# A column step of 144 instead of 128 in the gathered rows' two parts

## The chip, the cores and the metric

The kernel runs on one core of a Trainium2 chip. The metric is device time in microseconds (us), the median of several runs; lower is better. TensorE (PE) multiplies, and its weight loads are a row of their own in the profile (PEld). VectorE (DVE), ScalarE (ACT) and GpSimd (POOL) work on vectors, SyncE (SP) issues most transfers.

## The reference

One inference step of a decoder with two layers, for a prompt of 256 tokens and eight sample tokens (264 token columns), 1024 channels, float32. Layer 0 is a pooling mixer and a dense SwiGLU; a shared key and value projection follows; layer 1 is dilated attention and a mixture of eight SwiGLU experts, of which each token uses two. The change lies in the last part:

```python
def moe_swiglu(h, w_router, b_router, w1, w3, w2):
    ...
    for e in range(N_EXPERTS):
        y = swiglu(h, w1[e], w3[e], w2[e]).astype(jnp.float32)
        out = out + dense_gate[..., e:e + 1] * y
```

`swiglu` is `(silu(h @ w1) * (h @ w3)) @ w2`. An expert has two matrices of 1024 x 3584 and one of 3584 x 1024.

## The kernel before, in words

**Buffers.** Each buffer is placed by `sb`, one behind the other along the partition, its length rounded up to 64 bytes. A ring of seven slabs of 2048 columns takes the weights from memory (1 MB each). `w_hi` and `w_lo` have three slabs each of the same size. `tT` and its like hold 8 x 264 columns. `phase` has 12840 columns and is used by one stage after the other: `at` and `over` give names to parts of it.

**Split products.** Every float32 product is made of two parts of each operand. ACT rounds a weight slab from the ring into `w_hi` (L1266 for the experts), DVE writes the remainder into `w_lo` (L1734), and the helper `three` (L476 to L478) multiplies high by high, high by low and low by high into one sum: three matmuls, each with its own weight load. "Triple" is used below for these three.

**The expert stage.** For each expert a transfer on POOL's queue brings its 128 gathered rows (`xg`), PE transposes them in eight chunks of 128 columns (`turn_rows`, L907), ACT writes the high part `xe_hi` out of PSUM in two instructions of four chunks each (`gathered_high`, L1291), and DVE the remainder `xe_lo` (`gathered_low`, L1823). For the next expert this is done before the last products of the present one. Then, for each of seven column blocks j, `product` is called twice, for w1 and w3: eight chunks k, for each one triple with `xe_hi[:, k, :]` or `xe_lo[:, k, :]` as stationary operand and 512 columns of a weight slab as moving operand, all into one PSUM bank. `down` makes the product with w2 for the block before, with `upT_hi` and `upT_lo` (in `tT`) stationary, and alternates between two PSUM banks triple by triple. `turn` (L933) transposes the block `up` for it.

```python
                        for i in range(4):
                            k = 4 * half + i
                            mm = three(bank[bk][0:SLOTS, :], (xe_hi[:, k, :], xe_lo[:, k, :]), (hi[:, i, :], lo[:, i, :]), k == 0, k == KC - 1)
```

**Order and waits.** PE waits for `lo_done` of a slab; ACT waits for PE to be done with the slab whose place in `w_hi` it takes (`pair_used`); DVE waits for ACT; SP's transfer into a ring slot waits for DVE. At the start of an expert PE waits for `xe_ready`, which DVE gives after `xe_lo`.

**Earlier stages** use the same helper with the weights stationary and 264 token columns moving: `tHi` and `mLo` (8 chunks that stand 264 columns, 1056 bytes, apart), while the stationary slices `hi[:, k, ...]` stand 256 columns apart.

Of the kernel before, what the change touches and what calls it, by code (L numbers as in the profile page):

```python
# [6 lines left out]
F32R = mybir.dt.float32r  # L7
I32 = mybir.dt.int32
# [4 lines left out]
P = 128  # L13
D = 1024
KC = D // P
T = 256
NB = 8
# [10 lines left out]
NE = 8  # L28
# [7 lines left out]
SLOTS = 128  # L36
# [61 lines left out]
def yoco_step(nc, w, o):  # L98
# [25 lines left out]
    with ExitStack() as ctx:  # L124
# [3 lines left out]
        def sb(name, shape, dt=F32):  # L128

            n = 4  # L130
            for x in shape[1:]:
                n *= x
            placed[name] = free[0]
            free[0] += -(-n // 64) * 64
            return nc.alloc_sbuf_tensor_at(name, shape, dt, offset=placed[name])

        def over(name, other, skip, shape, dt):

            return nc.alloc_sbuf_tensor_at(name, shape, dt, offset=placed[other] + 4 * skip)
# [50 lines left out]
        phase = sb("phase", [P, PHASE])  # L190

        def at(offset, *shape):
            n = 1
            for s in shape:
                n *= s
            assert offset + n <= PHASE, (offset, shape)
            v = phase[:, offset:offset + n]
            if len(shape) == 2:
                v = v.rearrange("p (a b) -> p a b", a=shape[0])
            if len(shape) == 3:  # L200
                v = v.rearrange("p (a b c) -> p a b c", a=shape[0], b=shape[1])
            if len(shape) == 4:
                v = v.rearrange("p (a b c d) -> p a b c d", a=shape[0], b=shape[1], c=shape[2])
            return v
# [58 lines left out]
        htok = at(0, 3, D)  # L263
        x2tok = at(3072, 3, D)
        gtok = at(6144, 2, D)
        xe_hi = over("xe_hi", "phase", 8192, [P, KC, SLOTS], F32R)
        xe_lo = over("xe_lo", "phase", 9216, [P, KC, SLOTS], F32R)
        xg = hflat[:, 0:D]
        ye = mflat[:, 0:D]
        gsel = mflat[0:1 + NB, D:D + P]  # L270
        grow = at(10240, D)[0:1 + NB, :]

        upT_hi = [over(f"upT_hi{i}", "tT", 1024 * i, [P, 4, P], F32R) for i in range(2)]
        upT_lo = [over(f"upT_lo{i}", "tT", 1024 * i + 512, [P, 4, P], F32R) for i in range(2)]
        up_s = at(10240, 512)
        up = at(10752, 512)
        lg = at(11264, 3, NE)
        sel = at(11288, 3, NE)
        rank = at(11312, 3, NE)
        r_c = at(11336, 3, NE)  # L280
        gate = at(11360, 3, NE)
        picks = at(11384, 2, 3, NE)
        rowbase = at(11432, NE)
        rowsum = at(11440, 2, 3)
        r_s = at(11448, 3, 4)
        gpair = at(11464, 2, 3)
        r_a = at(11472, 3, NE, NE)
        r_b = at(11664, 3, NE, NE)
        row = over("row", "phase", 11864, [P, 2, 2, 3], I32)
        tail_s = at(11880, 3, 4)  # L290
        r_d = at(11896, 2, 3)
        rb_strip = at(11904, 1)

        pickT = over("pickT", "ada", 0, [P, NT], F32)[:, :]
        pick = at(11906, 3, P)
        xflat = xT[:, :, :].rearrange("p a b -> p (a b)")
        part = [xflat[:, 0:D], xflat[:, D:2 * D], over("part_s", "const", 0, [P, D], F32)[:, :]]
        early = [hflat[:, 0:D], hflat[:, D:2 * D]]
# [1792 lines left out]
```

## Time and profile before

| | us |
|---|---|
| median of 3 runs | 1690.21 (1689.18 to 1691.46) |
| the profiled execution | 1692.17 |
| its span, first to last instruction | 1689.9 |
| PE busy in the span | 1586.1 (94%) |
| DVE busy | 1256.4 (74%) |
| ACT busy | 982.8 (58%) |

A matmul's row has its start and a modelled end; neighbouring matmuls overlap in the rows, so the pace of PE is read from start to start, not from durations. The expert stage begins at about 705 us of the span and ends at about 1669.

### The profile page before, as it was taken

The numbers are of one execution on the slowest core, as the hardware profiler recorded it, in microseconds if no ns is written. First come the engines' busy times: TensorE is split into PE (matmuls) and PEld (weight loads), VectorE is DVE, ScalarE is ACT, GpSimd is POOL, SyncE is SP. The second block draws the span as 40 slices with busy tenths as digits, with TensorE's granted clock in tenths as the row PEclk, the third lists the DMA queues.
The fourth block names the chain that finished last, engine by engine and source line by source line (L and its number), as shares of the span: only waits on it lengthen the run. The fifth ranks groups of instructions, "written<-read, shape, count | busy, mean of one in ns | idle before, by whom it ended". The sixth has DMA issues, their size and how long they took to land.

```text
span 1689.9 us, 22932 instructions
## 1 busy us (share of the span) xinstructions
PE 1586.1 (94%) x8697; PEld 1296.3 (77%) x8697; DVE 1256.4 (74%) x1097; ACT 982.8 (58%) x885; POOL 152.2 (9%) x135
## 2 busy tenths in 40 slices
PE   6889999799899887799999999999999999999996
PEld 3579999498786674488888888888888888888874
DVE  4355543578784734488898888888888888889996
ACT  2244432433323524377877877877877877777774
POOL 0000000025542401200000000000000000000210
PEclk9789999899999888699999999999999999999998
DMA  9895545855458429599999999999999999999991
GB/s 346 296 345 178 178 158 187 295 179 187 162 206 302 151 75 350 199 333 380 358 395 385 357 395 381 365 385 374 376 389 370 377 376 374 385 375 373 394 387 48
DMA packets 248253, 512.28 MB, mean 303 GB/s; under 512 B 9045, under 2 KB 68613, under 8 KB 248175
## 3 DMA queue, kind: packets, MB, share of 16 engines
q1 hardware_dynamic: 241015, 490.27, 80.8%
q0 software_dynamic: 4768, 16.89, 2.5%
q10 hardware_dynamic: 2400, 4.17, 0.7%
q8 instruction: 45, 0.74, 0.2%
q14 instruction: 25, 0.20, 0.0%
HBM read 498.19 MB, written 13.82 MB: 303 GB/s over the span
## 4 chain that ended last, share of the span: by engine, by line
PE 77%; DVE 9%; DMA 4%; POOL 3%; ACT 3%; issue 3%; SPq 1%; DVEq 0%; ACTq 0%; POOLq 0%
PE wide L476 23%; PE wide L477 22%; PE wide L478 22%; DVE w_lo L1734 2%; POOL phase L1912 2%; DMA ring<-in_ada_mix_w 2%; DVE phase L1574 2%; DMA ring<-in_ada_ffn_w 1%; PE wide L933 1%; POOL phase L1918 1%; ACT w_hi L1266 1%; PE wide L527 1%; SPq L439 1%; PE wide L538 1%; PE wide L757 1%
## 5 line engine op out<-in xcount | busy, mean ns | idle before, releaser
L1734 DVE TENSOR_TENSOR w_lo<-ring,w_hi 128x2048 fp32r<-128x2048 f32 x336 | 767.6, 2290 | 113.9 <-ACT w_hi L1266 112.7
L1266 ACT ACTIVATE w_hi<-ring 128x2048 fp32r<-128x2048 f32 x336 | 643.5, 1919 | 216.0 <-PE wide L478 214.3
L476 PE MATMUL wide<-w_hi,xe_hi 128*128 128x512 f32 x896 | 356.0, 397 | 5.6 <-DVE w_lo L1734 2.9
L478 PE MATMUL wide<-w_hi,xe_lo 128*128 128x512 f32 x896 | 350.3, 391 | 0.0
L477 PE MATMUL wide<-w_lo,xe_hi 128*128 128x512 f32 x896 | 349.9, 391 | 0.0
L476 PE MATMUL wide<-tHi,w_hi 128*128 128x264 f32 x672 | 198.3, 295 | 20.4 <-DVE mLo L1492 20.4
L406 DVE TENSOR_TENSOR w_lo<-ring,w_hi 128x2048 fp32r<-128x2048 f32 (+1 forms) x58 | 139.6, 2410 | 100.1 <-ACT w_hi L1005 99.8
L477 PE MATMUL wide<-mLo,w_hi 128*128 128x264 f32 x736 | 212.1, 288 | 0.0
L476 PEld LDWEIGHTS wide<-w_hi,xe_hi 128*128 128x128 f32 x896 | 168.9, 189 | 44.9 <-DVE w_lo L1734 8.6
L478 PEld LDWEIGHTS wide<-w_hi,xe_lo 128*128 128x128 f32 x896 | 168.7, 188 | 36.1
L477 PEld LDWEIGHTS wide<-w_lo,xe_hi 128*128 128x128 f32 x896 | 169.0, 189 | 33.3
L478 PE MATMUL wide<-tHi,w_lo 128*128 128x264 f32 x672 | 192.8, 287 | 0.0
L476 PE MATMUL wide<-w_hi,upT_hi 128*128 128x512 f32 x448 | 177.1, 395 | 0.0
L477 PE MATMUL wide<-w_lo,upT_hi 128*128 128x512 f32 x448 | 176.0, 393 | 0.0
L478 PE MATMUL wide<-w_hi,upT_lo 128*128 128x512 f32 x448 | 174.3, 389 | 0.0
L476 PEld LDWEIGHTS wide<-tHi,w_hi 128*128 128x128 f32 x672 | 129.2, 192 | 30.2 <-issue 30.0
L1005 ACT ACTIVATE w_hi<-ring 128x2048 fp32r<-128x2048 f32 (+1 forms) x58 | 109.2, 1885 | 61.2 <-PE wide L478 61.1
L477 PEld LDWEIGHTS wide<-mLo,w_hi 128*128 128x128 f32 x736 | 141.9, 193 | 0.3
L478 PEld LDWEIGHTS wide<-tHi,w_lo 128*128 128x128 f32 x672 | 128.9, 192 | 0.0
L478 PEld LDWEIGHTS wide<-w_hi,upT_lo 128*128 128x128 f32 x448 | 84.1, 188 | 19.0
L476 PEld LDWEIGHTS wide<-w_hi,upT_hi 128*128 128x128 f32 x448 | 84.1, 188 | 18.3
L477 PEld LDWEIGHTS wide<-w_lo,upT_hi 128*128 128x128 f32 x448 | 84.3, 188 | 16.5
(313 smaller groups left out, 1711.6 us busy)
## 6 DMA issues: line engine op xcount, KB each, us to landing
ring<-in_moe_w SPq DMA_DIRECT2D x336, 1024.0 KB, 7.4
ring<-in_ffn_w SPq DMA_DIRECT2D x30, 1024.0 KB, 5.4
ring<-in_ada_mix_w SPq DMA_DIRECT2D x24, 1024.0 KB, 8.7
ring<-in_ada_ffn_w SPq DMA_DIRECT2D x24, 1024.0 KB, 11.9
ring<-in_w_q SPq DMA_DIRECT2D x12, 1024.0 KB, 9.2
ring<-in_cache_k SPq DMA_DIRECT2D x24, 512.0 KB, 5.0
ring<-in_cache_v SPq DMA_DIRECT2D x24, 512.0 KB, 6.5
ring<-in_w_kv SPq DMA_DIRECT2D x8, 1024.0 KB, 6.3
```

Source lines behind the costliest of these rows:

```text
L406: eng.tensor_tensor(w_lo[:, i % PAIRS, 0:size], ring[:, n % RING, 0:size], w_hi[:, i % PAIRS, 0:size].bitcast(F32), ALU.subtract).then_inc ...
L439: sp.dma_start(slab_view(n), slab_source(item)).then_inc(slab_in[n % RING], 16)
L476: pe.matmul(out, a[0], b[0], start=start, stop=False, skip_group_check=True)
L477: pe.matmul(out, a[0], b[1], start=False, stop=False, skip_group_check=True)
L478: return pe.matmul(out, a[1], b[0], start=False, stop=stop, skip_group_check=True)
L527: mm = pe.matmul(out[32 * k:32 * (k + 1), :], c32[:, 4 * half + k, :], slab_view(n)[:, k, :], start=(half == 0), stop=(half == 1))
L538: mm = pe.matmul(bank[7][:, 0:NT], ones, tT[:, k, :], start=(k == 0), stop=(k == KC - 1))
L1005: act.activation(w_hi[:, i % PAIRS, 0:size], ring[:, n % RING, 0:size], ACT.Copy).then_inc(hi_done, 1)
L1266: act.activation(w_hi[:, (NSPLIT + k) % PAIRS, :], ring[:, slot, :], ACT.Copy).then_inc(hi_done, 1)
L1574: ins = dve.tensor_tensor(k_prod[t % 2][:, cols], slab_view(n)[:, t % 2, cols], bank[6 + q], ALU.mult)
L1734: dve.tensor_tensor(w_lo[:, i, :], ring[:, slot, :], w_hi[:, i, :].bitcast(F32), ALU.subtract).then_inc(lo_done, 1)
L1912: pool.tensor_tensor(out, rawT[:, r % 4, :], cos, ALU.mult).then_inc(cos_done, 1)
```

## The change

`xe_hi` and `xe_lo` keep their shape, 8 chunks of 128 columns, but are cut from tiles with 144 columns to a chunk, so that chunk k begins 576 k bytes behind the first instead of 512 k. `xe_lo` and all that lies behind it in `phase` is moved up to make room; `xe_hi` begins where it did. `phase` keeps its size.

```diff
-        xe_hi = over("xe_hi", "phase", 8192, [P, KC, SLOTS], F32R)
-        xe_lo = over("xe_lo", "phase", 9216, [P, KC, SLOTS], F32R)
+        xe_hi = over("xe_hi", "phase", 8192, [P, KC, SLOTS + 16], F32R)[:, :, 0:SLOTS]
+        xe_lo = over("xe_lo", "phase", 9344, [P, KC, SLOTS + 16], F32R)[:, :, 0:SLOTS]
...
-        grow = at(10240, D)[0:1 + NB, :]
+        grow = at(10496, D)[0:1 + NB, :]
...
-        up_s = at(10240, 512)
-        up = at(10752, 512)
-        lg = at(11264, 3, NE)
...
+        up_s = at(10496, 512)
+        up = at(11008, 512)
+        lg = at(11520, 3, NE)
...
-        row = over("row", "phase", 11864, [P, 2, 2, 3], I32)
...
+        row = over("row", "phase", 12120, [P, 2, 2, 3], I32)
...
-        pick = at(11906, 3, P)
+        pick = at(12162, 3, P)
```

The places that are left out move by the same 256 columns.

## Rows read from the trace of the kernel before

**Rows 1.** The page, chain that ended last: by engine, by line.

```profile
PE 77%; DVE 9%; DMA 4%; POOL 3%; ACT 3%; issue 3%; SPq 1%; DVEq 0%; ACTq 0%; POOLq 0%
PE wide L476 23%; PE wide L477 22%; PE wide L478 22%; DVE w_lo L1734 2%; POOL phase L1912 2%; DMA ring<-in_ada_mix_w 2%; DVE phase L1574 2%; DMA ring<-in_ada_ffn_w 1%; PE wide L933 1%; POOL phase L1918 1%; ACT w_hi L1266 1%; PE wide L527 1%; SPq L439 1%; PE wide L538 1%; PE wide L757 1%
```

**Rows 2.** Windows, one per expert: busy time of each engine, granted clock, DMA share.

```profile
core 0: us, PE busy (x) PEld busy (x) DVE busy (x) ACT busy (x) POOL busy (x), PEclk, DMA share, GB/s
...
834.62:954.07 119.45, 119.20 (x542) 98.03 (x541) 105.64 (x60) 91.25 (x62) 1.08 (x2) 1.00 1.03 381
...
1551.30:1669.00 117.70, 115.94 (x520) 94.38 (x518) 104.62 (x62) 82.11 (x54) 19.24 (x10) 1.00 0.86 325
```

**Rows 3.** Waits in the second expert, 835 to 954 us.

```profile
engine line waited for: us in total, times, longest us
POOL y_rows L2009 <- DVE mT L1861: 129.3, 1, 129.3
ACT w_hi L1266 <- PE wide L478: 26.5, 37, 0.9
DVE w_lo L1734 <- ACT w_hi L1266: 14.1, 31, 1.2
...
PEld wide L476 <- DVE w_lo L1734: 0.9, 2, 0.7
...
PE wide L476 <- DVE w_lo L1734: 0.3, 1, 0.3
```

**Rows 4.** By tile, `xe_hi` and `xe_lo`: counts and durations.

```profile
engine op xcount: duration ns min/median/max, first and last start us, forms
L476 PE MATMUL wide<-w_hi,xe_hi x896: 389/389/791, 709.6 to 1656.1; 128*128 128x512 f32 x180
L477 PE MATMUL wide<-w_lo,xe_hi x896: 387/389/632, 710.2 to 1656.3; 128*128 128x512 f32 x180
L1291 ACT ACTIVATE xe_hi<-wide x16: 576/589/598, 707.0 to 1544.4; 128x512 fp32r<-128x512 f32 x16
L1823 DVE TENSOR_TENSOR xe_lo<-wide,xe_hi x16: 681/684/692, 708.1 to 1546.8; 128x512 fp32r<-128x512 f32 x16
...
L478 PE MATMUL wide<-w_hi,xe_lo x896: 388/389/632, 710.6 to 1656.6; 128*128 128x512 f32 x180
```

**Rows 5.** Timeline: start us, us, engine line operation; PE's transposes of gathered rows.

```profile
825.16 1.03 PE L907 MATMUL wide<-const,hT 128*128 128x128 f32 x8
```

**Rows 6.** Groups by line and form, expert stage: busy us, mean ns, idle before.

```profile
L907 PE MATMUL wide<-const,hT 128*128 128x128 f32 x56 | 7.2, 272 | 0.0
```

**Rows 7.** Groups by line and form, whole span, ACT and DVE.

```profile
L1154 ACT ACTIVATE phase<-wide 128x264 f32<-128x264 f32 x32 | 10.8, 389 | 53.4 <-PE wide L478 53.3
...
L1272 ACT ACTIVATE phase<-wide 128x256 f32<-128x256 f32 x8 | 3.1, 385 | 4.4 <-PE wide L849 4.1
...
L1273 ACT ACTIVATE phase<-wide 8x128 f32<-8x128 f32 x8 | 2.0, 250 | 0.0
...
L1377 DVE COPY phase<-wide 128x120 f32<-128x120 f32 x8 | 1.9, 283 | 1.2 <-PE wide L498 1.2
...
L1458 DVE COPY vec<-wide 128x96 f32<-128x96 f32 x1 | 0.3, 257 | 0.0
```

**Rows 8.** Timeline, boundary between the first and second expert.

```profile
827.18 1.07 ACT L1291 ACTIVATE xe_hi<-wide 128x512 fp32r<-128x512 f32 x2
...
829.52 1.28 DVE L1823 TENSOR_TENSOR xe_lo<-wide,xe_hi 128x512 fp32r<-128x512 f32 x2
...
831.30 0.19 PEld L476 LDWEIGHTS wide<-w_hi,xe_hi 128*128 128x128 f32 x1
```

**Rows 9.** Timeline of PE, settled product with `xe`: four triples apart.

```profile
835.62 0.39 PE L476 MATMUL wide<-w_hi,xe_hi 128*128 128x512 f32 x1
...
838.34 0.39 PE L476 MATMUL wide<-w_hi,xe_hi 128*128 128x512 f32 x1
```

**Rows 10.** Timeline of PE, product with `upT`: six triples apart.

```profile
826.72 0.39 PE L476 MATMUL wide<-w_hi,upT_hi 128*128 128x512 f32 x1
...
830.84 0.39 PE L476 MATMUL wide<-w_hi,upT_hi 128*128 128x512 f32 x1
```

**Rows 11.** Timeline of PE, 264 columns, layer 0: neighbouring triples.

```profile
201.41 0.28 PE L476 MATMUL wide<-tHi,w_hi 128*128 128x264 f32 x1
...
201.76 0.28 PE L476 MATMUL wide<-tHi,w_hi 128*128 128x264 f32 x1
...
202.13 0.29 PE L476 MATMUL wide<-tHi,w_hi 128*128 128x264 f32 x1
```

**Rows 12.** Timeline of PE, product with `xe` after a wait: successive triples.

```profile
840.12 0.50 PE L476 MATMUL wide<-w_hi,xe_hi 128*128 128x512 f32 x1 [0.25 <-DVE w_lo L1734]
...
840.92 0.40 PE L476 MATMUL wide<-w_hi,xe_hi 128*128 128x512 f32 x1
...
841.61 0.39 PE L476 MATMUL wide<-w_hi,xe_hi 128*128 128x512 f32 x1
...
842.30 0.39 PE L476 MATMUL wide<-w_hi,xe_hi 128*128 128x512 f32 x1
...
842.98 0.39 PE L476 MATMUL wide<-w_hi,xe_hi 128*128 128x512 f32 x1
```

**Rows 13.** Timeline of PE, 264 columns, query projection: eleven triples apart.

```profile
339.74 0.28 PE L476 MATMUL wide<-tHi,w_hi 128*128 128x264 f32 x1
...
343.73 0.28 PE L476 MATMUL wide<-tHi,w_hi 128*128 128x264 f32 x1
```

More of the change, by code:

```diff
@@ L270, in yoco_step @@
         gsel = mflat[0:1 + NB, D:D + P]
-        grow = at(10240, D)[0:1 + NB, :]
+        grow = at(10496, D)[0:1 + NB, :]
         upT_hi = [over(f"upT_hi{i}", "tT", 1024 * i, [P, 4, P], F32R) for i in range(2)]
         upT_lo = [over(f"upT_lo{i}", "tT", 1024 * i + 512, [P, 4, P], F32R) for i in range(2)]
-        up_s = at(10240, 512)
-        up = at(10752, 512)
-        lg = at(11264, 3, NE)
[L278 to L288, printed above, removed]
-        row = over("row", "phase", 11864, [P, 2, 2, 3], I32)
-        tail_s = at(11880, 3, 4)
-        r_d = at(11896, 2, 3)
-        rb_strip = at(11904, 1)
+        up_s = at(10496, 512)
+        up = at(11008, 512)
+        lg = at(11520, 3, NE)
+        sel = at(11544, 3, NE)
+        rank = at(11568, 3, NE)
+        r_c = at(11592, 3, NE)
+        gate = at(11616, 3, NE)
+        picks = at(11640, 2, 3, NE)
+        rowbase = at(11688, NE)
+        rowsum = at(11696, 2, 3)
+        r_s = at(11704, 3, 4)
+        gpair = at(11720, 2, 3)
+        r_a = at(11728, 3, NE, NE)
+        r_b = at(11920, 3, NE, NE)
+        row = over("row", "phase", 12120, [P, 2, 2, 3], I32)
+        tail_s = at(12136, 3, 4)
+        r_d = at(12152, 2, 3)
+        rb_strip = at(12160, 1)
         pickT = over("pickT", "ada", 0, [P, NT], F32)[:, :]
-        pick = at(11906, 3, P)
+        pick = at(12162, 3, P)
         xflat = xT[:, :, :].rearrange("p a b -> p (a b)")
```

## The prediction

> **What bounds the kernel now.** The page comes first. In the chain that ended last, TensorE holds 77%, and three lines of the same helper, L476 to L478, hold 67% [rows 1]. Those lines are the split products, three matmuls each, and the tiles that the change moves are their stationary operands in the expert stage. Then the windows, one expert to each: seven experts of 119.45 us and an eighth of some 118, at a granted clock of 1.00 (the 2.4 GHz level), with PE busy for 119.20 of 119.45 [rows 2]. Then the waits of one expert: the long ones run from the other engines to PE (ACT 26.5 us for `w_hi`'s buffer, DVE 14.1 for ACT), while PE's own waits for DVE are 0.9 and 0.3 us; POOL's 129.3 is on no path [rows 3]. So the expert stage, about 954 us, goes at the pace at which PE starts its matmuls. DMA is close behind: its share is 1.03 of the same windows [rows 2], so a faster PE would soon be held by the weights, and a slower PE is held by nothing.
>
> The view by tile gives the number of instructions concerned: 896 matmuls on each of the three lines have `xe_hi` or `xe_lo` as weights, 2,688 in all, each with its own weight load of 128 columns [rows 4].
>
> **What the change removes, adds and moves.** No instruction is added or removed and no wait. It alters (a) the addresses of the 2,688 weight loads, (b) the form in which ACT and DVE write the two tiles, and (c) the place of the tiles behind them.
>
> (c) first. Everything from `grow` on moves by 256 columns, 1024 bytes; `up`, which PE transposes, moves by as much. The transposes start 109 ns apart ((1.03 - 0.27) / 7, the eight of L907, which load the same number of columns; 0.27 is the length of one) [rows 5, 6]: that is the pace of a 128-column load, and a tile that stays contiguous gives no reason for another. I take 0. Bounds: 0 above and below, as no size, order or queue changes; the indirect transfers read their row numbers from another address of the same tile in the same number.
>
> (b) ACT's two writes of `xe_hi` take 589 ns each and DVE's two of `xe_lo` 684 [rows 4]. They become four runs of 128 columns with 16 between them. Rows for writes with gaps: ACT's copy into `htok`, two runs of 128 columns that stand 1024 apart, takes 385 ns for 256 columns, against 389 for 264 contiguous ones; DVE's copy with runs of 15 out of 16 takes 283 ns for 120 columns, against 257 for 96 contiguous ones, about 1 ns a column [rows 7]. Gaps cost nothing there, so I take 0. The cover: at the boundary between two experts, ACT is done with `xe_hi` at 828.25 and DVE with `xe_lo` at 830.80, and the first load of the new expert starts at 831.30 [rows 8]. So 0.50 us is free. From below nothing can be gained, because nobody waits for these writes at the seven boundaries between experts; ahead of the first expert PE does, and any difference there is paid once. From above: were a gap as dear as a whole new instruction (ACT's shortest here, 250 ns for 128 columns of 8 partitions [rows 7], three gaps, two writes), DVE's chain would grow by 1.5 us, 0.5 of it hidden; 1.0 us times 7 is 7 us. Queued behind DVE's write is the next `w_lo`, which PE would then meet late too. No row comes near this end.
>
> (a) The loads. A 128-column load can be repeated every 109 ns [rows 5, 6] and a matmul with 512 columns starts only every 227, so the length of a load does not count. What counts is that load and stream overlap. At 2.4 GHz 512 columns take 213.3 ns. With `xe` weights four triples take 838.34 - 835.62 = 2.72 us, 226.7 ns a matmul [rows 9]: 13.3 ns over the stream. With `upT` weights, same shapes, same moving slabs, six triples take 830.84 - 826.72 = 4.12 us, 228.9 ns a matmul [rows 10]: 15.6 over it. And in the earlier stage with 264 columns (110 ns), where the moving operand steps by 1056 bytes and the weights by 1024, triples of neighbouring chunks take 0.35 and 0.37 us [rows 11], a spread of 6%, with shapes and engines alike and nothing waiting. So a start address can alter the pace by a few ns.
>
> Where do `xe` and `upT` differ? Sizes summed from the kernel's text, each rounded up to 64 bytes: `tT`, in which `upT` lies, begins 24,576 + 24,576 + 7,872 + 3 x 8,448 = 82,368 bytes behind `w_hi`, which is 64 modulo 128; `phase` is 21,312 behind `tT`, and with 4 x 8192 `xe_hi` stands at 136,448, which is 0 modulo 128. Each of their chunks steps by 512 bytes and keeps this; the moving slices all begin at multiples of 512 from `w_hi`. Now `xe` steps by 576 bytes. Chunks 0, 2, 4, 6 stay at 0 modulo 128; chunks 1, 3, 5, 7 come to 64, where `upT` stands. `xe_lo` stands 4,608 bytes behind `xe_hi` instead of 4,096, both multiples of 512, so the two parts shift alike.
>
> If the address makes the whole difference, four chunks of eight pay 228.9 - 226.7 = 2.2 ns for each matmul: 1,344 x 2.2 = 3.0 us. But `upT` differs in a second way, that two PSUM banks alternate triple by triple, and the trace cannot part the two; then it is 0. I take the middle, 1.5 us, because both differ from `xe` in nothing else that I can see. For the ends I look further. Above: the triples after a wait of PE, before the pace has settled, start 0.69 and 0.69 us apart instead of 0.68 [rows 12], and the dearest triple of the 264 stage is 7 ns over its mean (0.37 against 3.99 / 11 = 0.363 [rows 11, 13]); were every triple 16 ns late, 896 x 16 = 14 us. Below: the 264 stage goes at 3.99 us for 33 matmuls, 120.9 each, 10.9 over its stream [rows 13]; were the 13.3 cut to this, 2,688 x 2.4 = 6.5 us.
>
> The Trainium skill, "SBUF — State Buffer", section "SBUF: two separate sides", says that full bandwidth asks only that consecutive accesses stay in a 16-byte line; 576 bytes are a whole number of such lines, so by it the change is worth 0 and the time 1690.2. The same section has PE waiting for no one at its ports; that agrees with the absence of any wait for another engine in the 264 stage, but not with triples of 0.35 and 0.37 there.
>
> **The sum.** Profiled execution: 1692.17 us, of which 1689.9 are the span. Plus 1.5 gives 1693.7. The profiled run lies 1.96 over the median of 1690.21, so on the scale of the medians it is 1690.21 + 1.5 = **1691.7**.
>
> **Rivals.**
> 1. *Slower: the pace never settles.* Place: each passage from one chunk to the next within a product. The 64-byte step puts load and stream into a new relation there, as a wait of PE does now, and the next triple pays what the first ones after a wait pay. 14 products x 8 experts x 7 passages = 784. At 4 ns each this is 3.1 us, the point from which it decides; at 8 ns, 6.3 us, 1696.5; at 16 ns, 12.5, 1702.7. For it: the settling of [rows 12] and the spread of [rows 11]. Against it: in the 264 stage the relation changes at each chunk too and the mean excess there is the smaller one. Nothing gives a slower PE its time back.
> 2. *Faster: the common step of 512 bytes is itself the cause of the 13.3 ns.* With the step broken the excess falls to the 10.9 of [rows 13]: -6.5 us, 1683.7; half of it, 1687.0. For it: that very stage, in which addresses drift. Against it: loads there fill nearly the whole matmul (109 of 121 ns), so the two excesses need not be the same thing; and DMA at a share of 1.03 would take back part.
> 3. *Writes with gaps are dear.* Up to 7 us, 1697, by (b); only if DVE's pair grows past 0.5 us.
>
> **How the numbers follow.** What a measurement here can tell from no change is about 0.2%, 3.4 us. The likeliest case, an alignment effect between 0 and 3.0 us, lies within it: 0.51, with a range of its own of 1689 to 1693.6. Rival 1 has 0.28 and rival 3 has 0.03, together 0.31 for slower. Rival 2 has 0.18. The range takes in rival 2 down to about three quarters of its gain and rival 1 up to 11 ns a passage: 1685 to 1699, leaving out some 0.09 at either end.
>
> **What would show it.** Mean start-to-start of `xe` triples in the steady part of a product: 0.68 for even and 0.69 for odd chunks if the forecast is right, 0.68 for all if the second difference of `upT` was the cause, over 0.69 at each passage for rival 1, under 0.68 for rival 2. Each expert's window should be 119.45 + 1.5 / 8 = 119.6 us. `upT` triples, ACT's 589, DVE's 684 and everything before 705 us should stand as they are. The prediction is wrong if the windows move by more than 0.4 us, or if time appears outside the expert stage.

## The result, and the profile after

The changed kernel takes 1698.67 us (median of 5 runs, 1698.07 to 1700.22) against 1690.91 for the kernel before (median of 5 as well, three of them those of the table). The ratio is 1.0054 with a 95% interval of 1.0043 to 1.0065: 7.8 us slower, clear of noise. The forecast was 1691.7, no change that a measurement could tell. The time lies just inside the range's upper end of 1699, which was set by rival 1 at 11 ns a passage; the likeliest case (1689 to 1693.6) was wrong.

The windows of the changed kernel, cut as in [rows 2] at the first `w_hi` of the chain in each expert (stretch, its length, busy time of each engine, granted clock, DMA share, GB/s):

```profile
834.26:954.93 120.67, 120.54 (x542) 98.15 (x541) 105.66 (x60) 91.25 (x62) 1.08 (x2) 1.00 1.01 374
954.93:1075.62 120.69, 120.56 (x542) 98.17 (x541) 105.66 (x60) 91.26 (x62) 1.07 (x2) 1.00 1.01 370
```

An expert takes 120.68 instead of 119.45 us, at the same granted clock, with the same number of instructions and the same busy time of DVE and ACT. Eight times 1.23 is 9.8 us, so the whole loss is in the expert stage and PE carries it. (The first matmul with `xe_hi` starts at 708.1 us of the span, in [rows 4] at 709.6; so the two spans, 1698.0 and 1689.9 us, differ by 8.1 only. No run tells why.) The prediction's own sign of being wrong, windows that move by more than 0.4 us, is met. The waits of the second expert, 835 to 955 us, answer to [rows 3]:

```profile
ACT w_hi L1266 <- PE wide L478: 27.7, 37, 0.9
DVE w_lo L1734 <- ACT w_hi L1266: 15.2, 31, 1.2
...
PEld wide L476 <- DVE w_lo L1734: 0.6, 1, 0.6
```

ACT waits 1.2 us longer for PE and DVE 1.1 us longer for ACT, while PE's own waits for DVE fall from 0.9 + 0.3 to 0.6 us: no new wait holds PE, it only starts its matmuls later. The timeline of PE (start us, duration, engine, line) in a product with `xe`, as [rows 9]:

```profile
834.60 0.40 PE L476 MATMUL wide<-w_hi,xe_hi 128*128 128x512 f32 x1
...
835.30 0.39 PE L476 MATMUL wide<-w_hi,xe_hi 128*128 128x512 f32 x1
835.53 0.39 PE L477 MATMUL wide<-w_lo,xe_hi 128*128 128x512 f32 x1
835.76 0.40 PE L478 MATMUL wide<-w_hi,xe_lo 128*128 128x512 f32 x1
835.99 0.40 PE L476 MATMUL wide<-w_hi,xe_hi 128*128 128x512 f32 x1
...
838.77 0.40 PE L476 MATMUL wide<-w_hi,xe_hi 128*128 128x512 f32 x1
```

Six triples take 838.77 - 834.60 = 4.17 us, 0.695 each, where [rows 9] has 0.68. The neighbour that was not moved, `upT`, as [rows 10]:

```profile
826.33 0.39 PE L476 MATMUL wide<-w_hi,upT_hi 128*128 128x512 f32 x1
...
830.45 0.39 PE L476 MATMUL wide<-w_hi,upT_hi 128*128 128x512 f32 x1
```

Six triples in 4.12 us, to the hundredth as before. And the writes with gaps, by tile, as [rows 4]:

```profile
L1291 ACT ACTIVATE xe_hi<-wide x16: 579/587/597, 705.5 to 1551.3; 128x512 fp32r<-128x512 f32 x16
L1823 DVE TENSOR_TENSOR xe_lo<-wide,xe_hi x16: 681/683/692, 706.6 to 1553.8; 128x512 fp32r<-128x512 f32 x16
```

They take 587 and 683 ns, before 589 and 684: the gaps cost nothing here.

Over the whole stage the triples of the gathered parts (start to start, those under 720 ns, in which no wait falls) have a mean of 694.3 ns against 681.8. Times 896 that is 11.2 us; some of it comes back, since a slower PE meets `w_lo` late less often (13 times instead of 27 in the view of the tile).

By chunk, medians of triple k in ns over the products of the stage, with the place of the chunk's weights against the moving slices, in bytes modulo 256 (worked out from the buffers' sizes):

```
chunk              0    1    2    3    4    5    6
before, place      0    0    0    0    0    0    0
before            686  680  680  680  680  680  680
after, place       0   64  128  192    0   64  128
after             696  695  695  697  698  695  694
```

(A triple here runs from the first matmul of chunk k to the first of chunk k + 1, so chunk 7 has none.) No chunk keeps its 680, not even chunks 0 and 4, whose place is still 0.

### The profile page after: what moved, and what is told of

Its sections match the earlier page's. It is cut to its first block, busy times and chain, and to the rows that moved or that the text cites. A ratio compares the mean times of both kernels' runs of the same rounds, so it can differ in the third digit from the quotient of the medians.

```text
span 1698.0 us, 22932 instructions
## 1 busy us (share of the span) xinstructions
PE 1598.4 (94%) x8697; PEld 1297.2 (76%) x8697; DVE 1256.5 (74%) x1097; ACT 982.7 (58%) x885; POOL 152.5 (9%) x135
## 3 DMA queue, kind: packets, MB, share of 16 engines
q10 hardware_dynamic: 2400, 4.17, 0.7%
## 4 chain that ended last, share of the span: by engine, by line
PE 79%; DVE 9%; DMA 3%; POOL 3%; ACT 3%; issue 3%; ACTq 0%; DVEq 0%; POOLq 0%
PE wide L476 23%; PE wide L477 22%; PE wide L478 22%; DVE w_lo L1734 2%; POOL phase L1912 2%; DVE phase L1574 2%; PE wide L527 1%; PE wide L538 1%; DMA ring<-in_ada_ffn_w 1%; PE wide L933 1%; POOL phase L1918 1%; ACT w_hi L1266 1%; PE wide L757 1%; PE wide L513 1%; DMA ring<-in_ada_mix_w 1%
## 5 line engine op out<-in xcount | busy, mean ns | idle before, releaser
L477 PE MATMUL wide<-w_lo,xe_hi 128*128 128x512 f32 x896 | 354.5, 396 | 0.0
L478 PE MATMUL wide<-w_hi,xe_lo 128*128 128x512 f32 x896 | 352.8, 394 | 0.0
L478 PEld LDWEIGHTS wide<-w_hi,xe_lo 128*128 128x128 f32 x896 | 168.8, 188 | 39.3
L478 PE MATMUL wide<-tHi,w_lo 128*128 128x264 f32 x672 | 192.8, 287 | 0.0
L478 PE MATMUL wide<-w_hi,upT_lo 128*128 128x512 f32 x448 | 175.9, 393 | 0.0
L478 PEld LDWEIGHTS wide<-tHi,w_lo 128*128 128x128 f32 x672 | 128.9, 192 | 0.0
L478 PEld LDWEIGHTS wide<-w_hi,upT_lo 128*128 128x128 f32 x448 | 84.1, 188 | 19.7
```

Source lines behind the costliest of these rows:

```text
L477: pe.matmul(out, a[0], b[1], start=False, stop=False, skip_group_check=True)
L478: return pe.matmul(out, a[1], b[0], start=False, stop=stop, skip_group_check=True)
```

## The experiments

All are against the kernel before; times are medians of 2 to 11 runs. The theories, as set down ahead of the first runs: *place* (the place of the weights against the moving slices, modulo 128 bytes, sets the pace), *passage* (a change of place from one load to the next costs) and *writes* (the gaps in ACT's and DVE's writes cost).

**1. Gaps in the writes, no new place.** The two parts interleaved, chunk by chunk.

```diff
-        xe_hi = over("xe_hi", "phase", 8192, [P, KC, SLOTS], F32R)
-        xe_lo = over("xe_lo", "phase", 9216, [P, KC, SLOTS], F32R)
+        xe_both = over("xe_both", "phase", 8192, [P, KC, 2 * SLOTS], F32R)
+        xe_hi = xe_both[:, :, 0:SLOTS]
+        xe_lo = xe_both[:, :, SLOTS:2 * SLOTS]
```

> Each chunk of the low part stands right behind its chunk of the high part, so the chunks of either are 256 columns (1024 bytes) apart and written in four runs with gaps, as in the changed kernel; every start keeps its place modulo 512 bytes against the moving slices. Writes theory (gaps in the writes are dear): the experts' windows grow as in the changed kernel, 120.7 us instead of 119.45, time about 1698.7. Place theory (the place of the weights modulo 128 bytes sets the pace) and passage theory (a change of place from one load to the next sets it): triples 0.680 us, windows 119.45, time as the kernel before, 1690.9 within 2.

1690.71 us, ratio 1.0011 (1.0000 to 1.0022). Its second expert:

```profile
833.22:952.67 119.45, 119.20 (x541) 98.06 (x540) 105.65 (x60) 91.23 (x61) 1.07 (x2) 1.00 1.02 378
```

119.45 us, as before, and triples of 0.680: the writes theory, rival 3, is out. A step as such does no harm either.

**2. A constant place, 64 bytes off.**

```diff
-        xe_hi = over("xe_hi", "phase", 8192, [P, KC, SLOTS], F32R)
-        xe_lo = over("xe_lo", "phase", 9216, [P, KC, SLOTS], F32R)
+        xe_hi = over("xe_hi", "phase", 8192 + 16, [P, KC, SLOTS], F32R)
+        xe_lo = over("xe_lo", "phase", 9344 + 16, [P, KC, SLOTS], F32R)
```

(The tiles behind them move as in the change; so in 6, 7, 9 and 11.)

> Both parts keep the step of 128 columns, but begin 16 columns (64 bytes) later, so that all chunks stand at 64 modulo 128 bytes, as upT does. Place theory: every settled triple goes from 0.680 to 0.687 us, 896 x 6.7 ns = 6 us, time about 1697. Passage theory in its plain form (only a changing place costs): triples stay at 0.680 to 0.687, never 0.69 and over in the settled part, and time lies between 1690.9 and 1697. If the 0.687 of upT comes from its two alternating PSUM banks alone: triples 0.680, time 1690.9.

1706.36 us, ratio 1.0104 (1.0087 to 1.0121): twice the loss of the change, though the place never changes within a product. PE's timeline:

```profile
834.45 0.40 PE L476 MATMUL wide<-w_hi,xe_hi 128*128 128x512 f32 x1
...
841.45 0.40 PE L476 MATMUL wide<-w_hi,xe_hi 128*128 128x512 f32 x1
```

Ten triples in 7.00 us, 0.700 each and not the 0.687 expected. So place counts, and more than was thought; passage in its plain form (never over 0.69) falls. `upT`, at its old place, runs at 0.687 in some products here and at 0.700 in others (mean about 694 ns). Two neighbouring products:

```profile
908.45 0.40 PE L476 MATMUL wide<-w_hi,upT_hi 128*128 128x512 f32 x1
...
913.35 0.40 PE L476 MATMUL wide<-w_hi,upT_hi 128*128 128x512 f32 x1
...
925.67 0.39 PE L476 MATMUL wide<-w_hi,upT_hi 128*128 128x512 f32 x1
...
930.48 0.39 PE L476 MATMUL wide<-w_hi,upT_hi 128*128 128x512 f32 x1
```

Seven triples take 4.90 us in the first (0.700 each) and 4.81 in the second (0.687). Of the 48 products with `upT` that run without a break, 25 hold the one rhythm, 23 the other, and none mixes them: one place can have two rhythms, and a product keeps the one it starts with.

A clash with ACT's or DVE's reads and writes does not show here: of PE's starts with `xe` behind the first two triples of a product, with no wait between, those with only ACT at work (196), only DVE (217) or both (1,464) all lie 233 ns apart in the mean.

**3. One gap in the middle.**

```diff
-        xe_hi = over("xe_hi", "phase", 8192, [P, KC, SLOTS], F32R)
+        xe_hi_t = over("xe_hi", "phase", 8192, [P, 2, 4 * SLOTS + 16], F32R)
+        xe_hi = [xe_hi_t[:, q, 0:4 * SLOTS].rearrange("p (k n) -> p k n", k=4) for q in range(2)]
...
```

> One gap of 16 columns, between chunk 3 and chunk 4 of each part, none elsewhere: chunks 0 to 3 at 0 modulo 128 bytes, chunks 4 to 7 at 64. Place theory: triples of chunks 0 to 3 take 0.680, of 4 to 7 0.687 us; 448 x 6.7 ns = 3 us, time about 1694. Passage theory: the triple at the gap and one or two after it take 0.69 to 0.70, those of chunks 0 to 2 and the last ones of 4 to 7 0.680 to 0.687; time 1692 to 1695. If what costs is not the gap but any departure from 128 columns for the whole tile, all eight are over 0.69 and the time is 1698.

1697.97 us, ratio 1.0055 (1.0038 to 1.0072). One product; the helper's first line is L478 here:

```profile
841.71 0.39 PE L478 MATMUL wide<-w_hi,xe_hi 128*128 128x512 f32 x1
...
844.44 0.39 PE L478 MATMUL wide<-w_hi,xe_hi 128*128 128x512 f32 x1
845.13 0.40 PE L478 MATMUL wide<-w_hi,xe_hi 128*128 128x512 f32 x1
845.83 0.39 PE L478 MATMUL wide<-w_hi,xe_hi 128*128 128x512 f32 x1
...
847.23 0.60 PE L935 MATMUL wide<-const,phase 128*128 128x128 f32 x4
```

Four triples ahead of the gap take 2.73 us (0.683 each), four behind it 2.79 (0.698). Medians of the triples over the stage: 698, 691, 680, 679 ns for chunks 0 to 3, 703, 698, 702 for 4 to 6. The place decides within one product, in the size of experiment 2. And a good place isn't at its 680 at once: coming from a bad one, chunk 0 and chunk 1 pay 18 and 11 ns first.

**4. `upT` moved to the good place.**

```diff
-        upT_hi = [over(f"upT_hi{i}", "tT", 1024 * i, [P, 4, P], F32R) for i in range(2)]
-        upT_lo = [over(f"upT_lo{i}", "tT", 1024 * i + 512, [P, 4, P], F32R) for i in range(2)]
+        upT_hi = [over(f"upT_hi{i}", "tT", 1024 * i + 16, [P, 4, P], F32R) for i in range(2)]
+        upT_lo = [over(f"upT_lo{i}", "tT", 1024 * i + 528, [P, 4, P], F32R) for i in range(2)]
```

> The kernel before with upT's four tiles 16 columns (64 bytes) later in tT, so that their chunks stand at 0 modulo 128 bytes against the moving slices, as the gathered rows' parts do. Place theory: upT's triples fall from 0.687 to 0.680 us, 448 x 6.7 ns = 3.0 us less, time about 1688. If the 0.687 comes from the two PSUM banks that alternate: upT's triples stay at 0.687 and the time at 1690.9.

1687.88 us, ratio 0.9994 (0.9984 to 1.0004). The timeline of PE with `upT`:

```profile
823.72 0.39 PE L476 MATMUL wide<-w_hi,upT_hi 128*128 128x512 f32 x1
...
827.80 0.39 PE L476 MATMUL wide<-w_hi,upT_hi 128*128 128x512 f32 x1
```

Six triples in 4.08 us, 0.680, though the two PSUM banks alternate as before: the 0.687 of [rows 10] was the place. An expert takes 119.14 us instead of 119.45. The time alone can't tell this gain from none.

**5. A step of 160 columns.** As the change, with `SLOTS + 32` and the rest moved on by as much.

> The changed kernel with a step of 160 columns instead of 144: 640 bytes, so that every chunk stands at 0 modulo 128 bytes, but no longer at one place modulo 512. Place theory with a period of 128 bytes: all triples 0.680 us, windows 119.45, time as the kernel before. If the period is 256 or 512: 128 and 384 are new places, half the chunks leave 0.680, as with 144, and the time lies near 1698. Passage theory (any step that is no multiple of 512 costs): 1698 too.

1699.81 us, ratio 1.0060 (1.0037 to 1.0082).

```profile
833.91 0.39 PE L476 MATMUL wide<-w_hi,xe_hi 128*128 128x512 f32 x1
...
840.87 0.39 PE L476 MATMUL wide<-w_hi,xe_hi 128*128 128x512 f32 x1
```

Ten triples in 6.96 us, 0.696: 0 modulo 128 is not enough. The period is longer, or passages cost after all; experiments 9 and 10 part these.

**6 and 7. Constant places 32 and 16 bytes off.** As 2, with 8 and with 4 columns in place of 16.

> Step of 128 columns, both parts 8 columns (32 bytes) later: all chunks at 32 modulo 128. Place theory: a pace of its own, the same for all chunks, between 0.680 (at 0) and 0.700 (measured at 64) if the cost grows with the distance, so near 0.690 and 1698; below 0.680 would be a better place than the one of the kernel before.

> Step of 128 columns, both parts 4 columns (16 bytes) later: all chunks at 16 modulo 128. Place theory with growth by distance: near 0.685 a triple and 1694. If only 64 modulo 128 is a bad place: 0.680 and 1690.5.

32 bytes: 1702.55 us, ratio 1.0074 (1.0045 to 1.0103), mean triple 699.6 ns. 16 bytes: 1697.54 us, ratio 1.0033 (1.0010 to 1.0056), with a mean triple of 691.4 ns. Two neighbouring products of the run with 16 bytes:

```profile
912.19 0.39 PE L476 MATMUL wide<-w_hi,xe_hi 128*128 128x512 f32 x1
...
916.95 0.39 PE L476 MATMUL wide<-w_hi,xe_hi 128*128 128x512 f32 x1
...
918.77 0.40 PE L476 MATMUL wide<-w_hi,xe_hi 128*128 128x512 f32 x1
...
922.97 0.40 PE L476 MATMUL wide<-w_hi,xe_hi 128*128 128x512 f32 x1
```

Seven triples of 0.680 us in the first, six of 0.700 in the second: again two rhythms, each held through a product. From the second triple on, 46 of the 112 products stay near 680, 61 near 700, and 5 change between. It was expected that the cost grows with the distance; it does not, it is there at once, and at 16 bytes only in some products. No place came out under 680.

**8. Everything moved together.**

```diff
+        pad = sb("pad", [P, 16])
         w_hi = sb("w_hi", [P, PAIRS, SLAB], F32R)
```

> The kernel before with 64 unused bytes ahead of the split weights' buffers: moving slices, gathered parts and upT all move by 64 bytes, and keep their places against each other. If the place of the weights against the moving slices counts: triples of the gathered parts 0.680, of upT 0.687, time as the kernel before, 1690.5. If the place in memory itself counts: the gathered parts come to 64 modulo 128, as in the run with both parts 16 columns later, triples 0.700 and 1706, and upT comes to 0, triples 0.680.

1689.51 us, ratio 1.0001 (0.9989 to 1.0012).

```profile
830.71:950.21 119.50, 119.24 (x541) 98.03 (x540) 105.62 (x60) 91.57 (x61) 1.07 (x2) 1.00 1.01 375
```

119.50 us an expert, triples of 0.680 and, with `upT`, 0.687. A move of everything by 64 bytes does not matter, one of the weights alone does: what counts is the place against the moving slices, not the place in memory.

**9. A constant place, 128 bytes off.** As 2, with 32 columns.

> Step of 128 columns, both parts 32 columns (128 bytes) later: all chunks at 128 modulo 256, one constant place. Place theory with a period of 256 bytes (as the run with a step of 640 bytes asks for it): 128 is a bad place of its own, triples 0.69 to 0.70, time 1697 to 1702. Passage theory (a constant place is good where it is a multiple of 128, and the 640 bytes cost because the place changes at every chunk): triples 0.680, time 1690.5.

1704.49 us, ratio 1.0091 (1.0072 to 1.0109).

```profile
833.84 0.40 PE L476 MATMUL wide<-w_hi,xe_hi 128*128 128x512 f32 x1
...
840.84 0.40 PE L476 MATMUL wide<-w_hi,xe_hi 128*128 128x512 f32 x1
```

Ten triples in 7.00 us. 128 bytes off is a bad place by itself.

**10. A step of 192 columns.**

```diff
-        xe_hi = over("xe_hi", "phase", 8192, [P, KC, SLOTS], F32R)
-        xe_lo = over("xe_lo", "phase", 9216, [P, KC, SLOTS], F32R)
+        xe_hi = over("xe_hi", "phase", 8192, [P, KC, SLOTS + 64], F32R)[:, :, 0:SLOTS]
+        xe_lo = over("xe_lo", "shared", 96, [P, KC, SLOTS + 64], F32R)[:, :, 0:SLOTS]
```

> Step of 192 columns (768 bytes): the chunks stand by turns at 256 and at 0 modulo 512 bytes, two places at which constant steps gave 0.680 (the gathered parts of the kernel before, and upT moved by 64 bytes); the low part lies in another buffer at the same place modulo 512. Place theory: 0.680 throughout, 1690.5. Passage theory: the place changes by 256 bytes at every chunk, so 0.69 and over in all eight, about 1698.

1690.06 us, ratio 0.9996 (0.9986 to 1.0006).

```profile
833.93 0.39 PE L476 MATMUL wide<-w_hi,xe_hi 128*128 128x512 f32 x1
...
838.01 0.39 PE L476 MATMUL wide<-w_hi,xe_hi 128*128 128x512 f32 x1
```

Six triples in 4.08 us, 0.680, with a place that changes by 256 bytes at every chunk. With 9 this gives the place theory with a period of 256 bytes, as far as it was tried (0 and 256 modulo 512 are alike), and the passage theory falls as the whole cause.

**11. The low part alone, 64 bytes off.** `xe_hi` as before, `xe_lo` as in 2.

> Step of 128 columns; the high part at its old place (256 modulo 512), the low part alone 64 bytes off it. One load of three is at a bad place, and the place changes twice in each triple. Place theory, load by load: a third of the 20 ns, 0.687 a triple, 1696. Passage theory: no settled rhythm, 0.69 to 0.70 and 1698 to 1706.

1698.72 us, ratio 1.0048 (1.0033 to 1.0063).

```profile
833.74 0.39 PE L476 MATMUL wide<-w_hi,xe_hi 128*128 128x512 f32 x1
...
839.29 0.39 PE L476 MATMUL wide<-w_hi,xe_hi 128*128 128x512 f32 x1
```

Eight triples in 5.55 us, 0.694, a steady rhythm with median gaps of 228, 229 and 236 ns. One load of three at the bad place costs 13 of the 20 ns, not a third: the loads don't add up one by one, and the place theory's sum for it was wrong. Its time lies in the passage theory's range too, and 10 speaks against that theory only for steps of 256 bytes: that passages between a good and a bad place cost something of their own is left open.

**12. The version of 4, measured again.**

> The kernel before with upT moved by 64 bytes, once more with more rounds, as the version that may beat both: from the triples of its first run (0.680 instead of 0.687, 448 of them) 3.0 us less than the kernel before, a ratio of 0.9982. If other waits take the gain back: 1.0000.

1688.18 us, ratio 0.9989 (0.9980 to 0.9998): by the ratio 1.9 us faster than the kernel before (by the medians, 1689.27 and 1688.18, 1.1), less than the 3.0 of its triples, and the best ratio of all versions. The interval only just leaves out no change.

## Why the prediction was wrong

**What stood.** PE sets the pace of the expert stage, a slower PE is held by nothing, no instruction changes, writes with gaps are free, and the place of a load against the moving stream alters the pace. The time outside the stage did not grow, and `upT`'s triples stayed. That the time fell inside the range is in part luck: the upper end was rival 1's, and its mechanism is not the main one.

**The step that failed** is (a), in three points.

- *The period.* "Chunks 0, 2, 4, 6 stay at 0 modulo 128" and so at 0.680. The period is 256 (9 and 10). Chunks 2 and 6 come to 128, as bad as 64; only 0 and 4 have a good place. I had two places in the trace, 0 and 192 modulo 256, and took the smallest period that parts them.
- *The size.* The odd chunks were given `upT`'s 2.2 ns a matmul. A wholly shifted product pays (700 - 680) / 3 = 6.7 (experiment 2). `upT`'s 192 mostly has a milder rhythm than 32, 64 and 128, and it was the only other place that I had read from the trace for this shape.
- *The middle.* Half the difference was put down to the PSUM banks. Experiment 4 gives the place the whole of it. (There was a third difference, which I overlooked: `down` uses each chunk of `upT` for two triples running. Experiment 4 leaves that as it was, too.)

In the terms of the sum: 1.5 us was forecast; the mean triple grew by 12.5 ns, 11.2 us for 896 of them, of which the windows keep 9.8 and the medians 7.8. Constant places alone, taken chunk by chunk, would give the changed kernel triples of (680 + 700 + 700 + 687) / 4 = 692 ns in the mean, an estimate from [rows 9, 10] and experiments 2 and 9; 694 were measured. The same sum gives 690 for experiment 5, which has 696. So the places make most of the loss, and the rest goes with the change between unlike places; no run takes it by itself.

**Rival 1** (0.28) had the side and nearly the price, 4 to 16 ns a triple, but not the mechanism: it laid the cost on the passage between chunks, and passages by 256 bytes are free (10) while a constant bad place costs most of all (2). Its sign, triples over 0.69, is what the trace shows, but a bad place gives the same sign. What is right in it is the settling: in experiment 3 two triples pass before a good place has its pace. That chunks 0 and 4 of the changed kernel take 696 and 698 agrees with it, as a bad place follows after one triple, and so do the good places of experiment 5 (medians of 694 to 696). **Rival 2**, a faster pace from a broken step, found no support: none of the places tried lies under 0.680. **Rival 3** fell with experiment 1.

The rule of the Trainium skill that the prediction weighed ("SBUF — State Buffer", section "SBUF: two separate sides"), by which an access that crosses to a new 16-byte line pays, would have the change at 0. 576 bytes are whole lines and the change costs 7.8 us; the measurement decides.

**Open** are why the period is 256 bytes (and whether places other than 0 repeat with it), why one place can have two rhythms, what a change between unlike places costs by itself, and whether moving the streamed slices alone acts the same way.

## What to carry to other kernels

Where full-rate matmuls each load new weights, read the pace from start to start of equal matmuls, and compare it between tiles: two constant paces for one shape, with nothing waiting, can come from the operands' places, as they did here. Here the stationary tile belongs at a multiple of 256 bytes from the moving one, and in every chunk: pad to that, or not at all. Before a trace with two places is turned into a rule, ask which periods would fit the same two points.

## What was not expected of the hardware

- The place of weights against the stream: 0 modulo 256 bytes 0.680 us a triple; 32, 64 and 128 0.698 to 0.700; 192 (`upT`) 0.687, or 0.700 in some products, above all in experiment 2; 16 either 0.680 or about 0.70. Everything moved by 64 bytes: no difference (8).
- A matmul of 512 columns with a weight load of its own starts 226.7 ns after the one before at the best place and 233.3 at the bad ones, at a granted clock of 1.00 (the 2.4 GHz level): 13.3 and 20 ns over the 213.3 of 512 columns at one a cycle. The Trainium skill, "TensorE: Matmul & The Clock Gate", section "Back-to-back issue gap", gives an isolated gap at the higher clock as the columns at 2.4 GHz plus 2.5 ns; no run here comes down to that.
- After a bad place the pace took two triples, about 1.4 us, to settle (698, 691, 680 ns in experiment 3).
